# First softmax attention: the factors of every third job ahead of the next job's maxima on VectorE

## The chip, the cores and the metric

One Trainium2 chip, one core of it. The kernel runs the whole computation in one launch. The metric is the device time of one execution in microseconds (us); smaller is better. The core has TensorE (matmuls and transposes), VectorE, ScalarE, GpSimd, and SyncE, which here issues the DMAs. Each engine works through its own queue in order; they wait for each other by semaphores.

## The reference

A block of two mixer layers (256 tokens, width 1024) and a second block with two other attentions and a feed-forward part. What matters here is layer 0, a sparse attention with 16 heads of 64 and 4 key groups:

```python
o_cmp = softmax over 15 compressed keys
o_slc = softmax over the selected blocks      # 256 tokens: all 4 blocks are selected, so causal
o_win = softmax over a window of 512          # 256 tokens: causal
o = gates[0] * o_cmp + gates[1] * o_slc + gates[2] * o_win
return (o * silu(z)) @ w_out
```

So two causal softmax attentions over 256 keys (two "branches") and a small one, gated and added. Then follow `x = x + y`, the norm and layer 1.

## The kernel before, in words

Every weight goes from memory into a raw buffer (SyncE's queue), is split by ScalarE into a high half (`w_hi`, L1242) and by VectorE into the rest (`w_lo`, L1688), and TensorE does three matmuls for each product (L458 to L460).

The first softmax attention (`attention`, called between the gate projection `a_z` and the output projection `a_out`) is cut into 24 jobs, `JOBS`. Three jobs belong to each pair of heads: tokens 128 to 255 for branch 0, the same for branch 1, and tokens 0 to 127 for both branches. A job fills one PSUM bank of 512 columns: two rows of 256 keys in the first two kinds, four rows of 128 keys in the third (job numbers j with j % 3 == 2). It goes through these steps; the letters are used throughout:

- S(j), TensorE, L601 and L604: scores into a bank. It waits until the exponentials of job j-3 or so have left the bank.
- M(j), VectorE, L1805: the negated row maxima, one reduction of 512 columns.
- E(j), ScalarE, L1345: two exponentials of 256 columns, or four of 128 in each third job, each with a read of its accumulated sum.
- F(j), VectorE, L1815 and L1817: the factors, a reciprocal of the sums and a product with the gates (2 or 4 columns).
- W(j), GpSimd, L2446: the probabilities times the factors, 512 columns.
- T(j), TensorE, L616: four transposes; then a copy out of PSUM, by ScalarE (L1335) for two jobs of three and by VectorE (L1872) for the third.
- V(j), TensorE, L650: probabilities times values, two jobs at a time.

All engines run the same loop over turns j. In turn j TensorE issues S(j), T(j-3) and in every second turn two V. ScalarE issues the copy of job j-3 and then E(j). VectorE issues M(j) first and then F(j-1), and behind them what else stands in that turn: the compressed branch's softmax (L1826 to L1845, in turns 0 to 5), the copy of its transposed weights (L1866), the copy of each third job (L1872), the gated output (L1790) and its rest half (L1795) once in six turns, and the split of a weight piece (L1688) in a few turns. The order is written by hand, and no scheduler changes it. GpSimd issues only the W, in order.

What each engine waits for around the change: M(j) for S(j) (`s_ready`), E(j) for M(j) (`s_max`) and for T(j-3), whose buffer it takes, F(j) for E(j) (`p_exp`), W(j) for F(j) (`p_fac`), T(j) for W(j) (`p_ready`). In ScalarE's queue these lines hold it:

```python
act.wait_ge(S["s_max"], j + 1)
if j >= 3:
    act.wait_ge(S["pt_ps"], j - 2)
```

Of the kernel before, what the change touches and what calls it, by code (L numbers as in the profile page):

```python
# [152 lines left out]
def program(nc, io, out):  # L153
# [7 lines left out]
    with ExitStack() as ctx:  # L161
# [177 lines left out]
        def bc(ap, shape, at):  # L339
            return ap.unsqueeze(at).broadcast_to(shape)  # L340
# [9 lines left out]
        NJ = len(JOBS)  # L350
# [4 lines left out]
        def z_done(j):  # L355
            return 5 + min(max(j - 7, 0) // 3, 3)
# [6 lines left out]
        def score_bank(j):  # L363
            return ps[2 + j % 2 if j < J4 else (j - J4) % 4]
# [4 lines left out]
        def quad_at(j):  # L369
            q, r = divmod(j - JQ - LAG - 1, JQ)  # L370
            return q if r == 0 and 0 <= q < 4 else None
# [1298 lines left out]
        def _(dve):  # L1670
# [4 lines left out]
            def link(ins):  # L1675

                chain[0] += 1
                ins.then_inc(S["dve"], 1)
                dve.wait_ge(S["dve"], chain[0])

            def split_lo_to(n):

                while nxt[0] < min(n, NSUB):
                    s = nxt[0]
                    dve.wait_ge(S["hi_ready"], s + 1)
                    if slot_free(s):
                        dve.wait_ge(S["sub_used"], slot_free(s))
                    V.tensor_tensor(split(w_lo, s), rawsub(s)[0], split(w_hi, s).bitcast(F), ALU.subtract).then_inc(S["lo_ready"], 1)  # L1688
                    nxt[0] += 1
# [90 lines left out]
            def z_gate(phase, f):  # L1780

                dve.wait_ge(S["z_t"], 8 * phase + f + 1)
                V.scalar_tensor_tensor(out=zs[:, f, :], in0=zs[:, f, :], scalar=1.0, in1=z_bank(phase, f)[:, 0:T], op0=ALU.add, op1=ALU.mult)\
                    .then_inc(S["z_free"], 1)

            def gated(q):

                o = ps[6 + q % 2][:, :].rearrange("p (a n) -> p a n", a=2)
                g = og[:, 2 * q:2 * q + 2, :]
                V.tensor_tensor(g, o, zs[:, 2 * q:2 * q + 2, :], ALU.mult).then_inc(S["og_ready"], 1)  # L1790

            def output_lo(phase, q):
                dve.wait_ge(S["ot_hi"], 4 * phase + q + 1)
                for f in (2 * q, 2 * q + 1):
                    V.tensor_tensor(tok_tiles(1, f), og[:, f, :].rearrange("p (a b) -> p a b", b=P), tok_tiles(0, f).bitcast(F), ALU.subtract)\  # L1795
                        .then_inc(S["ot_lo" if f % 2 else "dve"], 1)
                chain[0] += 1

            def attention(z0):

                def maxima(j):
                    qt, heads, brs = JOBS[j]
                    nb, c = 4 // (qt + 1), 4 * (j % 8)
                    dve.wait_ge(S["s_ready"], j + 1)
                    V.tensor_reduce(nmax[:, c:c + nb], score_bank(j)[:, :].rearrange("p (r n) -> p r n", r=nb), X, ALU.max, negate=True)\  # L1805
                        .then_inc(S["s_max"], 1)

                def factors(j):

                    qt, heads, brs = JOBS[j]  # L1810
                    nb, c = 4 // (qt + 1), 4 * (j % 8)
                    dve.wait_ge(S["p_exp"], j + 1)
                    f, sm_ = facs[:, c:c + nb], sums[:, c:c + nb]
                    h = heads[0]
                    link(V.reciprocal(f, sm_))  # L1815
                    fv = f.rearrange("p (h b) -> p h b", b=len(brs))
                    V.tensor_tensor(fv, fv, gate[:, qt, 1 + brs[0]:2 + brs[-1], h:h + 2].rearrange("p b h -> p h b"), ALU.mult).then_inc(S["p_fac"], 1)  # L1817

                pcv = pc.rearrange("p (h c) -> p h c", c=16)

                def compressed_sums():
                    dve.wait_ge(S["cm_s"], 1)
                    for qt in range(2):
                        hi_s, lo_s = (ps[4 + qt][:, :].rearrange("p (h i c) -> p h i c", h=NH, i=2)[:, :, i] for i in range(2))
                        o = pc[:, T * qt:T * qt + T].rearrange("p (h c) -> p h c", c=16)
                        link(V.tensor_tensor(o, hi_s, bc(cst[:, C_CB + 16 * qt:C_CB + 16 * qt + 16], [P, 16, 16], 1), ALU.add))  # L1826
                        link(V.tensor_tensor(o, o, lo_s, ALU.add))

                def compressed_maxima():
                    link(V.tensor_reduce(cmx, pcv, X, ALU.max))  # L1830

                def compressed_shift():
                    V.tensor_tensor(pcv, pcv, bc(cmx, [P, 32, 16], 2), ALU.subtract).then_inc(S["cm_sub"], 1)

                def compressed_factors():
                    dve.wait_ge(S["cm_exp"], 1)
                    link(V.tensor_reduce(csum, pcv, X, ALU.add))
                    link(V.reciprocal(cf0, csum))
                    for qt in range(2):
                        some_seen = cst[:, C_CM + 16 * qt:C_CM + 16 * qt + 1]  # L1840
                        f = cf0[:, NH * qt:NH * qt + NH]
                        link(V.scalar_tensor_tensor(out=f, in0=f, scalar=some_seen, in1=gate[:, qt, 0, :], op0=ALU.mult, op1=ALU.mult))

                def compressed_weights():
                    V.tensor_tensor(pcv, pcv, bc(cf0, [P, 32, 16], 2), ALU.mult).then_inc(S["cm_p"], 1)  # L1845

                for j in range(NJ + LAG + 3):
                    if j < NJ:
                        maxima(j)
                    if 1 <= j <= NJ:  # L1850
                        factors(j - 1)
                    if j in (1, 3):
                        z_gate(0, 6 + j // 2)
                    if j == 0:
                        compressed_sums()
                    elif j == 1:
                        compressed_maxima()
                    elif j == 2:
                        compressed_shift()
                    elif j == 4:  # L1860
                        compressed_factors()
                    elif j == 5:
                        compressed_weights()
                    if j == 7:
                        dve.wait_ge(S["cm_pt"], 1)
                        V.tensor_copy(pcT, ps[5][:, :]).then_inc(S["cm_ptsb"], 1)  # L1866
                    v = j - LAG
                    if 0 <= v < NJ and v % 3 == 2:
                        dve.wait_ge(S["pt_ps"], v + 1)
                        if v >= 4:  # L1870
                            dve.wait_ge(S["pv"], v - 3)
                        V.tensor_copy(xn[:, 512 * (v % 4):512 * (v % 4) + 512], ps[4 + v % 2][:, :]).then_inc(S["pt_dve"], 1)  # L1872
                    q = quad_at(j)
                    if q is not None:
                        if q == 0:
                            dve.wait_ge(S["z_free"], 8)
                        dve.wait_ge(S["pv"], JQ * (q + 1))
                        gated(q)
                    q = quad_at(j - 1)
                    if q is not None:  # L1880
                        output_lo(0, q)
                    split_lo_to(z0 + z_done(j - 1) + RING)
# [212 lines left out]
            split_lo_to(za + 9)  # L2095
            z_gate(0, 5)
            attention(za)
            norm_stage(1, first["a_out"])

# [438 lines left out]
```

## Time and profile before

| | |
|---|---|
| median of 3 runs | 792.64 us (792.53 to 792.73) |
| the profiled execution | 793.19 us |
| its span, first to last instruction | 791.3 us |
| granted TensorE clock, mean | 0.999 |
| TensorE busy | 773.3 us, 98% |
| VectorE busy | 545.6 us, 69% |
| ScalarE busy | 423.4 us, 54% |
| GpSimd busy | 109.2 us, 14% |

The first attention takes about 53 us of the span, from S(0) at 105.5 us to the last V at 159.0 us. The chain of waits, followed back from the last instruction, is TensorE's for 83% of the span and VectorE's for 8%. Rows of the timeline give start and duration of an instruction, and in brackets how long its engine had been idle before it and who ended that.

### The profile page before, as it was taken

Reading aid. Unit: us, or ns where it says so; the run is one execution under the profiler, and the core shown is the slowest. Engines: PE = TensorE matmul, PEld = TensorE weight load, DVE = VectorE, ACT = ScalarE, POOL = GpSimd, SP = SyncE. Lnnn points to the kernel's source line nnn. Section 1 sums busy time; section 2 is a strip of 40 time slices with the busy share of each in tenths; the row PEclk is TensorE's granted clock in tenths of the full one; section 3 lists DMA queues with packets and bytes.
Section 4 is the critical chain, followed back from the end, with each engine's and each line's share of the span. In section 5 each row is a group of like instructions: output and inputs, shape, how many; then the busy total and the mean of one; then the engine's idle time right before and its main releaser. Section 6 shows DMA issues by size and latency. Waiting matters only on the chain.

```text
span 791.3 us, 13449 instructions
## 1 busy us (share of the span) xinstructions
PE 773.3 (98%) x5250; PEld 678.5 (86%) x5250; DVE 545.6 (69%) x912; ACT 423.4 (54%) x832; POOL 109.2 (14%) x105
## 2 busy tenths in 40 slices
PE   7999999999999999999999999999999999999996
PEld 4888998788998788999977999999987888888885
DVE  5897978857986763449439577778766656666565
ACT  5447557845548644457356355654445444454453
POOL 1344125501725020000000000111001000000000
PEclk9999999999999999999999999999999999999999
DMA  8756311144431543744335443327464555545631
GB/s 298 231 169 214 107 54 54 55 158 145 160 107 55 190 137 125 263 146 128 104 107 191 145 146 107 118 97 236 166 218 153 185 188 195 204 160 197 215 121 53
DMA packets 93106, 120.74 MB, mean 153 GB/s; under 512 B 8490, under 2 KB 69347, under 8 KB 93044
## 3 DMA queue, kind: packets, MB, share of 16 engines
q1 hardware_dynamic: 92176, 117.67, 44.4%
q0 software_dynamic: 432, 1.57, 0.6%
q8 instruction: 42, 0.69, 0.3%
q10 hardware_dynamic: 436, 0.65, 0.2%
q14 instruction: 20, 0.16, 0.1%
HBM read 118.83 MB, written 1.05 MB: 151 GB/s over the span
## 4 chain that ended last, share of the span: by engine, by line
PE 83%; DVE 8%; ACT 4%; issue 2%; POOL 1%; DMA 1%; ACTq 0%; POOLq 0%; DVEq 0%
PE banks L458 19%; PE banks L460 18%; PE banks L459 18%; PE banks L510 9%; PE banks L512 4%; DVE w_lo L1688 3%; PE banks L530 1%; PE banks L650 1%; PE banks L568 1%; PE banks L1091 1%; PE banks L604 1%; ACT w_hi L1242 1%; PE banks L616 1%; DMA cst<-in_c_keep 1%; ACT tmp L1382 1%
## 5 line engine op out<-in xcount | busy, mean ns | idle before, releaser
L1688 DVE TENSOR_TENSOR w_lo<-raw,w_hi 128x1024 fp32r<-128x1024 f32 x210 | 260.7, 1252 | 101.8 <-ACT w_hi L1242 101.3
L1242 ACT CAST w_hi<-raw 128x1024 fp32r<-128x1024 f32 (+1 forms) x211 | 218.5, 1046 | 150.4 <-PE banks L460 116.7
L458 PE MATMUL banks<-h,w_hi 128*128 128x256 f32 (+1 forms) x512 | 149.6, 292 | 0.7 <-DVE ar L2146 0.4
L460 PE MATMUL banks<-h,w_lo 128*128 128x256 f32 (+1 forms) x512 | 145.3, 284 | 0.0
L459 PE MATMUL banks<-h,w_hi 128*128 128x256 f32 (+1 forms) x512 | 145.3, 284 | 0.0
L458 PE MATMUL banks<-w_hi,h 128*128 128x512 f32 (+1 forms) x264 | 104.3, 395 | 0.9 <-DVE h L1695 0.6
L460 PE MATMUL banks<-w_hi,h 128*128 128x512 f32 (+1 forms) x264 | 102.2, 387 | 0.0
L459 PE MATMUL banks<-w_lo,h 128*128 128x512 f32 (+1 forms) x264 | 102.1, 387 | 0.0
L510 PE MATMUL banks<-h,w_hi 128*128 128x512 f32 x288 | 100.5, 398 | 0.0
L458 PEld LDWEIGHTS banks<-h,w_hi 128*128 128x128 f32 x512 | 97.6, 191 | 3.2 <-issue 2.0
L459 PEld LDWEIGHTS banks<-h,w_hi 128*128 128x128 f32 x512 | 97.7, 191 | 0.2
L460 PEld LDWEIGHTS banks<-h,w_lo 128*128 128x128 f32 x512 | 97.6, 191 | 0.0
L512 PE MATMUL banks<-h,w_lo 128*128 128x256 f32 x252 | 70.7, 281 | 0.0
L2419 POOL TENSOR_TENSOR small<-small 128x2 f32<-128x2 f32 (+5 forms) x26 | 26.8, 1030 | 297.0 <-DVE small L2404 184.3
L458 PEld LDWEIGHTS banks<-w_hi,h 128*128 128x128 f32 x264 | 50.2, 190 | 13.1 <-issue 3.0
L510 PEld LDWEIGHTS banks<-h,w_hi 128*128 128x128 f32 x288 | 52.4, 188 | 10.1
L460 PEld LDWEIGHTS banks<-w_hi,h 128*128 128x128 f32 x264 | 50.2, 190 | 10.1
L459 PEld LDWEIGHTS banks<-w_lo,h 128*128 128x128 f32 x264 | 50.3, 190 | 9.2
L512 PEld LDWEIGHTS banks<-h,w_lo 128*128 128x128 f32 x252 | 47.6, 189 | 1.5
L458 PE MATMUL banks<-w_hi,o 128*128 128x512 f32 x88 | 34.4, 391 | 0.3 <-DVE w_lo L1688 0.3
L460 PE MATMUL banks<-w_hi,o 128*128 128x512 f32 x88 | 34.2, 389 | 0.0
L459 PE MATMUL banks<-w_lo,o 128*128 128x512 f32 x88 | 34.2, 389 | 0.0
(352 smaller groups left out, 1359.5 us busy)
## 6 DMA issues: line engine op xcount, KB each, us to landing
raw<-in_w_in SPq DMA_DIRECT2D x24, 1024.0 KB, 5.0
raw<-in_a_w_in SPq DMA_DIRECT2D x13, 1024.0 KB, 5.1
raw<-in_w_ffn_gate SPq DMA_DIRECT2D x11, 1024.0 KB, 5.0
raw<-in_w_ffn_up SPq DMA_DIRECT2D x11, 1024.0 KB, 5.1
raw<-in_w_ffn_down SPq DMA_DIRECT2D x11, 1024.0 KB, 4.9
raw<-in_b_w_in SPq DMA_DIRECT2D x9, 1024.0 KB, 5.0
raw<-in_w_gate SPq DMA_DIRECT2D x8, 1024.0 KB, 5.3
raw<-in_a_w_out SPq DMA_DIRECT2D x4, 1024.0 KB, 4.9
```

The costliest lines, as they stand in the source:

```text
L458: mm(o, lh, rh, start=start, stop=False)
L459: mm(o, lh, rl, start=False, stop=False)
L460: return mm(o, ll, rh, start=False, stop=stop)
L510: last = mm(o, wh[:, kt, :], both(kt), start=kt == 0, stop=kt == KT - 1, skip_group_check=True)
L512: mm(o[:, 0:T], wl[:, kt, :], rhs_h(kt), start=False, stop=False, skip_group_check=True)
L530: last = nc.tensor.transpose(ps[4 + 2 * tt + half][:, P * j:P * j + P], xn[:, a:a + P], ident)
L568: last = nc.tensor.transpose(tbank(phase, e)[:, P * j:P * j + P], t, ident)
L604: last = mm(b[:, wide * i:wide * i + wide], q_st[:, h // 2, h % 2, P * qt:P * qt + P], k[:, h // 4, brs[0]:brs[-1] + 1, 0:w], start=False, ...
L616: last = nc.tensor.transpose(ps[4 + j % 2][:, P * i:P * i + P], tmp[:, 512 * (j % 3) + P * i:512 * (j % 3) + P * i + P], ident)
L1242: nc.scalar.copy(split(w_hi, s), rawsub(s)[0]).then_inc(S["hi_ready"], 1)
L1688: V.tensor_tensor(split(w_lo, s), rawsub(s)[0], split(w_hi, s).bitcast(F), ALU.subtract).then_inc(S["lo_ready"], 1)
L2419: G.tensor_tensor(dst, var, mhalf[0:var.shape[0], 0:n], ALU.pow).then_inc(S[done], 1)
```

## The change

In turns 3, 6, 9, ... 24 VectorE issues F(j-1) ahead of M(j) rather than behind it. F(j-1) is there the factors of a job with four exponentials. In all other turns the order stays M(j), F(j-1). In turn 24 there is no M.

```diff
                 for j in range(NJ + LAG + 3):
+                    if j and j % 3 == 0 and j <= NJ:
+                        factors(j - 1)
                     if j < NJ:
                         maxima(j)
-                    if 1 <= j <= NJ:
+                    if j % 3 and j <= NJ:
                         factors(j - 1)
```

VectorE's queue around turn 15, in the kernel before. The rows are F13, the copy of job 11, the split of a weight piece, M15, F14, M16 and F15:

```order
L1815 RECIPROCAL small<-small 128x2 [waits p_exp]
L1817 TENSOR_TENSOR small<-small 128x2 [waits dve]
L1872 COPY xn<-banks 128x512 [waits pv,pt_ps]
L1688 TENSOR_TENSOR w_lo<-raw,w_hi 128x1024 [waits sub_used,hi_ready]
L1805 TENSOR_REDUCE small<-banks 128x2 [waits s_ready]
L1815 RECIPROCAL small<-small 128x4 [waits p_exp]
L1817 TENSOR_TENSOR small<-small 128x4 [waits dve]
L1805 TENSOR_REDUCE small<-banks 128x2 [waits s_ready]
L1815 RECIPROCAL small<-small 128x2 [waits p_exp]
L1817 TENSOR_TENSOR small<-small 128x2 [waits dve]
```

The same place in the changed kernel (lines below the edit count two more):

```order
L1815 RECIPROCAL small<-small 128x2 [waits p_exp]
L1817 TENSOR_TENSOR small<-small 128x2 [waits dve]
L1874 COPY xn<-banks 128x512 [waits pv,pt_ps]
L1688 TENSOR_TENSOR w_lo<-raw,w_hi 128x1024 [waits sub_used,hi_ready]
L1815 RECIPROCAL small<-small 128x4 [waits p_exp]
L1817 TENSOR_TENSOR small<-small 128x4 [waits dve]
L1805 TENSOR_REDUCE small<-banks 128x2 [waits s_ready] x2
L1815 RECIPROCAL small<-small 128x2 [waits p_exp]
L1817 TENSOR_TENSOR small<-small 128x2 [waits dve]
```

F14, the pair with 128x4, stands ahead of M15, and M15 and M16 follow each other.

VectorE's queue around turn 21, in the kernel before: the copy of job 17, M21, F20, M22, F21 and the gated output of a quarter of the heads:

```order
L1872 COPY xn<-banks 128x512 [waits pv,pt_ps]
L1805 TENSOR_REDUCE small<-banks 128x2 [waits s_ready]
L1815 RECIPROCAL small<-small 128x4 [waits p_exp]
L1817 TENSOR_TENSOR small<-small 128x4 [waits dve]
L1805 TENSOR_REDUCE small<-banks 128x2 [waits s_ready]
L1815 RECIPROCAL small<-small 128x2 [waits p_exp]
L1817 TENSOR_TENSOR small<-small 128x2 [waits dve]
L1790 TENSOR_TENSOR ar<-banks,ar 128x512 [waits pv]
```

The same place in the changed kernel:

```order
L1874 COPY xn<-banks 128x512 [waits pv,pt_ps]
L1815 RECIPROCAL small<-small 128x4 [waits p_exp]
L1817 TENSOR_TENSOR small<-small 128x4 [waits dve]
L1805 TENSOR_REDUCE small<-banks 128x2 [waits s_ready] x2
L1815 RECIPROCAL small<-small 128x2 [waits p_exp]
L1817 TENSOR_TENSOR small<-small 128x2 [waits dve]
L1790 TENSOR_TENSOR ar<-banks,ar 128x512 [waits pv]
```

M21 now stands behind F20, and with it behind the wait for job 20's exponentials.

The queues of TensorE, ScalarE, GpSimd and SyncE are the same in both kernels.

## Rows read from the trace of the kernel before

**Rows 1.** The page: busy time by engine, share of the span, instructions.

```profile
PE 773.3 (98%) x5250; PEld 678.5 (86%) x5250; DVE 545.6 (69%) x912; ACT 423.4 (54%) x832; POOL 109.2 (14%) x105
```

**Rows 2.** Busy time of the stretch: length, PE, PEld, DVE, ACT, POOL, clock, DMA share, GB/s.

```profile
105.00:159.00 54.00, 51.43 (x484) 45.32 (x482) 42.41 (x107) 41.45 (x157) 25.71 (x24) 1.00 0.12 41
```

**Rows 3.** Timeline of TensorE: start, duration, what, idle time before and its releaser.

```profile
121.07 0.63 PE L624 MATMUL banks<-cst,ar 128*128 128x128 f32 x4 [1.36 <-ACT xn L1335]
...
141.26 0.66 PE L616 MATMUL banks<-cst,tmp 128*128 128x128 f32 x4 [0.87 <-POOL tmp L2446]
...
148.86 0.61 PE L616 MATMUL banks<-cst,tmp 128*128 128x128 f32 x4
```

**Rows 4.** The chain of waits, 140 to 160 us: start, duration, what.

```profile
140.17 1.05 POOL tmp L2446
...
151.31 0.69 DVE small L1805
...
155.83 1.05 POOL tmp L2446
```

**Rows 5.** Timeline of ScalarE and VectorE, turns 3, 6 and 9.

```profile
113.89 0.21 ACT L1345 ACTIVATION_READ_ACCUMULATOR tmp<-banks,small 128x1 f32 x1
...
114.07 0.69 DVE L1805 TENSOR_REDUCE small<-banks 128x2 f32<-128x512 f32 x1 [0.64 <-PE banks L604]
...
114.99 0.48 ACT L1345 ACTIVATE tmp<-banks,small 128x256 f32<-128x256 f32 x1
...
120.24 0.21 ACT L1345 ACTIVATION_READ_ACCUMULATOR tmp<-banks,small 128x1 f32 x1
...
120.30 0.68 DVE L1805 TENSOR_REDUCE small<-banks 128x2 f32<-128x512 f32 x1
...
124.83 0.37 ACT L1345 ACTIVATE tmp<-banks,small 128x128 f32<-128x128 f32 x1 [1.16 <-DVE small L1805]
...
128.68 0.59 ACT L1335 COPY xn<-banks 128x512 f32<-128x512 f32 x1 [0.94 <-PE banks L616]
```

**Rows 6.** Timeline of VectorE and ScalarE, turn 12: M12, F11, E12, the copy behind.

```profile
133.47 0.68 DVE L1805 TENSOR_REDUCE small<-banks 128x2 f32<-128x512 f32 x1
134.07 0.16 DVE L1815 RECIPROCAL small<-small 128x4 f32<-128x4 f32 x1
...
134.35 0.68 DVE L1805 TENSOR_REDUCE small<-banks 128x2 f32<-128x512 f32 x1
...
134.19 0.47 ACT L1345 ACTIVATE tmp<-banks,small 128x256 f32<-128x256 f32 x1 [0.65 <-DVE small L1805]
...
135.10 0.58 ACT L1335 COPY xn<-banks 128x512 f32<-128x512 f32 x1
```

**Rows 7.** Timeline of VectorE, turn 15: M15 and F14.

```profile
139.12 0.68 DVE L1805 TENSOR_REDUCE small<-banks 128x2 f32<-128x512 f32 x1
139.72 0.16 DVE L1815 RECIPROCAL small<-small 128x4 f32<-128x4 f32 x1
```

**Rows 8.** Timelines, turn 18: M18, F18, E18, and W17 with W18.

```profile
145.51 0.68 DVE L1805 TENSOR_REDUCE small<-banks 128x2 f32<-128x512 f32 x1
...
147.28 0.17 DVE L1815 RECIPROCAL small<-small 128x2 f32<-128x2 f32 x1 [0.20 <-ACT tmp L1345]
...
146.22 0.47 ACT L1345 ACTIVATE tmp<-banks,small 128x256 f32<-128x256 f32 x1 [0.54 <-DVE small L1805]
...
146.55 2.20 POOL L2446 TENSOR_TENSOR tmp<-tmp,small 128x512 f32<-128x512 f32 x2 [2.71 <-DVE small L1817]
```

**Rows 9.** Timelines of ScalarE and VectorE, turn 21: E20's first and last part, M21, F21.

```profile
148.76 0.37 ACT L1345 ACTIVATE tmp<-banks,small 128x128 f32<-128x128 f32 x1
...
150.05 0.21 ACT L1345 ACTIVATION_READ_ACCUMULATOR tmp<-banks,small 128x1 f32 x1
...
149.56 0.68 DVE L1805 TENSOR_REDUCE small<-banks 128x2 f32<-128x512 f32 x1
...
151.91 0.15 DVE L1815 RECIPROCAL small<-small 128x2 f32<-128x2 f32 x1
```

## The prediction

> **What bounds the kernel now.** First the page. TensorE is busy 98% of the span [rows 1], so time is lost only where TensorE ends up waiting, or where something beside it sets the end of a stretch. Then the table by stretch: the first attention lies at 105 to 159 us, and TensorE is busy 51.43 of 54 us there, 95%, at the full granted clock (1.00) [rows 2]. Third, the timeline of TensorE in that stretch: it stands idle 1.36 us at 121.07, behind the ScalarE copy of job 3, and 0.87 us at 141.26, behind GpSimd's W14 [rows 3]. T18 at 148.86 starts the moment W18 is done: almost no slack. Last, the chain of waits: through 141 to 151 us it runs on TensorE, but at 151.31 it goes over to VectorE (M22) and stays with VectorE and GpSimd up to W23 at 155.83 [rows 4]. So the change, which leaves TensorE's work alone, counts (a) where it moves one of the waits of rows 3, and (b) undiluted at the end, where the chain is VectorE's own queue.
>
> **Unit prices.** An M holds VectorE for 0.60 us and E starts 0.72 us after its M (133.47 to 134.07, and to 134.19) [rows 6]. An F, two tiny instructions, holds VectorE 0.28 us (134.07 to 134.35) [rows 6]. W starts 0.45 us behind its F and takes 1.05 us (139.72, 140.17) [rows 4, 7]. Four exponentials last from 148.76 to 150.05 + 0.21 = 150.26, 1.50 us [rows 9]; two take 1.04 us by the same pattern, and ScalarE is free for the next 0.91 us after their start (134.19 to the copy at 135.10) [rows 6].
>
> **What the change does.** Nothing is added or removed. In turns 3, 6, ... 21 (seven places; in turn 24 there is no M, so nothing moves) F(j-1) goes ahead of M(j). If E(j-1) has ended by then, F comes 0.60 us earlier and M 0.28 later. If not, VectorE now stands and waits for E(j-1), with M(j) queued behind that wait; and since E(j) needs M(j), ScalarE stands too. No DMA is moved; SP's queue is not passed. GpSimd's and ScalarE's orders are as they were. The times below are those of the trace of before plus the shift.
>
> Turn 3: E2 ends at 113.89 + 0.21 = 114.10, and M3 began at 114.07 [rows 5]. Now F2 at 114.13, M3 at 114.41, E3 at 115.13 instead of 114.99 [rows 5]: **0.14 late**. E3, the compressed exponentials, VectorE's compressed factors, M5, E5 and the copy of job 3 follow without a gap up to TensorE's 1.36 us wait [rows 3], so TensorE and all behind it are 0.14 late. I leave this out of the times of the next turns and add it at the end.
>
> Turn 6: E5 ends at 120.24 + 0.21 = 120.45, M6 began at 120.30 [rows 5]. Now M6 at about 120.76, E6 and E7 0.5 to 0.6 late. ScalarE was idle for 1.16 us before E8 [rows 5], which waits for M8, and M8 for TensorE: that swallows it. The copy of the compressed weights, queued behind F6 at 122.34, is as late, and T5 at 123.91 needs it done (123.02): room for 0.9. **Nothing**; without that cover it would cost 0.6. Turn 9: F8 cannot go before E8 has ended (it waited for it before too, at 126.37), so W8 gains nothing and M9, E9 are some 0.7 late; ScalarE's idle 0.94 us before the copy of job 7 [rows 5] swallows that. **Nothing**; uncovered 0.7.
>
> Turn 12: VectorE comes to M12 at 133.47 straight from a weight split, E11 long done. F11 goes first, M12 and E12 are 0.28 late [rows 6]. From E12 on ScalarE has no gap (E12, copy, E13, a weight cast, E14), and VectorE's weight split, which waits for that cast, ends at 139.12 where M15 starts [rows 7]: now 139.40. **0.28 late** on the ScalarE/VectorE side. TensorE's T12 goes 0.27 late with W12, but this is hidden in the 0.87 us wait of T14.
>
> Turn 15: E14 now ends at 139.23, F14 starts at 139.40 instead of 139.72 [rows 7], W14 at 139.85 instead of 140.17, and T14 at 140.94 instead of 141.26: TensorE **gains 0.32**. But M15 is at 139.68, 0.56 late, and so are E15, E16, the cast and the next split. The Trainium skill's page "Perfetto Trace Analysis", section "Optimization Strategy", says to find the gaps on the engine to be filled and "determine how to make those dependencies start sooner". By that rule W14 ought to give up to 0.60 of the 0.87 us gap; the rows give 0.32, and it doesn't stay. It is the third rival below.
>
> Turn 18: VectorE comes to M18 at 145.51 + 0.56 = 146.07; F17 first, M18 at 146.35, E18 at 147.07 (was 146.22): 0.85 late [rows 8]. F17 is no earlier than before. F18, which waits for E18, goes from 147.28 to 148.12 [rows 8]; W18 was right behind W17 and ended at 146.55 + 2.20 = 148.75, and now ends at 148.12 + 0.45 + 1.05 = 149.62. T18 goes from 148.86 to 149.65: TensorE **0.79 late**, the gain is gone. E20 had waited a little for M20; it now starts as soon as E19 leaves ScalarE, at 149.37 instead of 148.76 (0.61 late), and ends at 150.87.
>
> Turn 21: M21 ran at 149.56, in the shadow of E20 [rows 9]. Now F20 waits to 150.90, M21 starts at 151.18 (1.62 late), E21 at 151.90, ending at 152.94. F21, which had run at 151.91 [rows 9], waits for that until 152.97: **1.06 late**. S22 is 0.79 late and gives M22 at 152.10, no later bound. Behind F21 VectorE's queue (gated output, M23, F22, copy, output halves, F23) and then W23 are the chain of waits with nothing in reserve [rows 4], so W23 is at 156.89 and the output projection 1.06 late.
>
> **Sum:** 0.14 + 1.06 = **1.2 us slower**. After the section the projection is bound by TensorE, with the weights fetched ahead, so the delay stays as it is. The profiled execution took 793.19 us for a span of 791.3; I expect a span of 792.5, and 792.64 + 1.2 = 793.84 for the median. The price of an F in a new place is bounded by 0.16 us (one instruction alone) and 0.45 (its whole latency); at three to four turns that count, the sum lies between 0.8 and 1.7; I take 0.28, the measured pitch.
>
> **Rivals.** *Only the end counts:* the slack at turns 12 to 18 is larger than I read, and E20 is on time. Then F20 is at 150.29, M21 at 150.57, E21 ends at 152.33, F21 at 152.36: 0.45 late, with turn 3's 0.14 some 0.6 in all, 793.2. For it: ScalarE's small idle times at M14, M16 and M20; against: the weight cast and split in turns 12 to 17 run without any. *More is lost:* the covers of turns 6 and 9 don't hold. The place is E9: it now ends at about 128.4, and F9 stands at 128.85. From 0.4 us more lateness on, F9 and the chain behind it up to W9 and the splits are late as well, with 0.6 to 0.7 per turn: 1.2 + 0.6 to 1.3 = about 2.2 (1.7 to 2.6), 794.8. For it: VectorE was busy almost to the next M in these turns; against: the two idle times of rows 5. *Faster:* earlier W are what TensorE wants, the 0.87 us gap goes, and the M side is hidden. It would bring 0.3 (turn 15 as worked out) to 0.9 (all of the gap), 792.0. For it: rows 3; against: in turns 9, 18 and 21 F comes no earlier at all, for it is the exponentials it waits for. That the order doesn't come out as the diff says can't be: VectorE runs its queue as written, and the listing shows it.
>
> **How the numbers follow.** Forecast 0.51 (its own range 0.8 to 1.7 us), only the end 0.20, more lost 0.22, faster 0.07. 0.2% is 1.6 us, about what a measurement tells from no change. The forecast lies within it but for a tenth, "only the end" wholly, "more lost" beyond it, and "faster" mostly within, since the gap on TensorE is under 1 us: faster 0.03, same 0.69, slower 0.28. The range leaves out the gain, the low part of "only the end" and the top of "more lost": 792.9 to 795.0.
>
> **What would show it.** In the new profile: M21 about 1.6 us later than before, right after E20's end; ScalarE idle about 0.7 us between the copy of job 18 and E21; T14's wait down from 0.87 to under 0.5 us; a new wait of TensorE of some 0.8 us for W18 before T18; F2 ahead of M3 and E3 0.1 late. Weight splits and matmuls outside the section as before. Wrong would be: T18 on time, M22 still the place where the chain goes over to VectorE, or a shift that differs between W23 and the end of the program.

## The result and the profile after

The changed kernel takes 793.87 us (median of 21 runs, 793.46 to 794.57), the kernel before 792.63 us (21 runs, 792.29 to 793.38). The ratio is 1.0016, with an interval of 1.0011 to 1.0022: 1.2 us slower, and clear of the noise, though under the 0.2% that was called no change.

| | before | after |
|---|---|---|
| median | 792.63 us | 793.87 us |
| span of the profiled execution | 791.3 us | 792.1 us |
| M0, the first maxima of the section | 106.41 | 105.98 |
| W23, the last weighting | 155.83 | 156.67 |
| from M0 to W23 | 49.42 us | 50.69 us |

The two profiled executions don't reach the section at the same time: M0 is 0.43 us earlier in the one after, although nothing ahead of it differs. So all shifts below are counted from M0. From M0 to W23 the changed kernel takes 1.27 us more, and 1.27 - 0.43 = 0.84 is what the spans differ by (0.8). After W23 nothing is added or won back.

The page of the changed kernel, first lines: busy times are those of before [rows 1], to within 0.3 us on each engine.

```profile
span 792.1 us, 13449 instructions
...
PE 773.3 (98%) x5250; PEld 678.2 (86%) x5250; DVE 545.8 (69%) x912; ACT 423.5 (53%) x832; POOL 109.0 (14%) x105
...
PE 81%; DVE 10%; ACT 4%; issue 3%; POOL 1%; DMA 1%; ACTq 0%; POOLq 0%; DVEq 0%
```

The last line is the chain of waits: TensorE's share fell from 83% to 81%, VectorE's rose from 8% to 10%.

Timeline of VectorE and ScalarE in the changed kernel, turns 3 and 9 (they answer to [rows 5]): F2, M3, E3; then F8, M9, E9 and the copy of job 7.

```profile
113.71 0.18 DVE L1815 RECIPROCAL small<-small 128x4 f32<-128x4 f32 x1 [0.71 <-ACT tmp L1345]
...
114.00 0.69 DVE L1805 TENSOR_REDUCE small<-banks 128x2 f32<-128x512 f32 x1
...
114.72 0.47 ACT L1345 ACTIVATE tmp<-banks,small 128x256 f32<-128x256 f32 x1
...
126.10 0.18 DVE L1815 RECIPROCAL small<-small 128x4 f32<-128x4 f32 x1 [0.70 <-ACT tmp L1345]
...
126.39 0.68 DVE L1805 TENSOR_REDUCE small<-banks 128x2 f32<-128x512 f32 x1
...
127.11 0.48 ACT L1345 ACTIVATE tmp<-banks,small 128x256 f32<-128x256 f32 x1 [0.57 <-DVE small L1805]
...
128.41 0.59 ACT L1335 COPY xn<-banks 128x512 f32<-128x512 f32 x1 [0.28 <-PE banks L616]
```

Here is the new wait: VectorE stands 0.70 us at F8 with M9 behind it, then ScalarE stands 0.57 us for M9. But ScalarE still waits 0.28 us for TensorE before the copy of job 7 (0.94 before): the delay stops there.

VectorE, turns 12, 15, 18, and W18 on GpSimd (they answer to [rows 6 to 8]). "x2" is two maxima in a row.

```profile
133.20 0.16 DVE L1815 RECIPROCAL small<-small 128x4 f32<-128x4 f32 x1
133.40 0.17 DVE L1817 TENSOR_TENSOR small<-small 128x4 f32<-128x4 f32 x1
133.48 1.28 DVE L1805 TENSOR_REDUCE small<-banks 128x2 f32<-128x512 f32 x2
...
139.14 0.17 DVE L1815 RECIPROCAL small<-small 128x4 f32<-128x4 f32 x1
139.34 0.17 DVE L1817 TENSOR_TENSOR small<-small 128x4 f32<-128x4 f32 x1
139.42 1.28 DVE L1805 TENSOR_REDUCE small<-banks 128x2 f32<-128x512 f32 x2
...
146.10 1.28 DVE L1805 TENSOR_REDUCE small<-banks 128x2 f32<-128x512 f32 x2
...
148.31 1.04 POOL L2448 TENSOR_TENSOR tmp<-tmp,small 128x512 f32<-128x512 f32 x1 [1.01 <-DVE small L1817]
```

Counted from M0, M12 is 0.44 late, M15 0.73, M18 1.02: 0.29 more each time, on top of the 0.15 of turn 3.

TensorE in the changed kernel (it answers to [rows 3]): the compressed weights, T12, T14, T18.

```profile
120.80 0.63 PE L624 MATMUL banks<-cst,ar 128*128 128x128 f32 x4 [1.47 <-ACT xn L1335]
...
136.79 0.66 PE L616 MATMUL banks<-cst,tmp 128*128 128x128 f32 x4 [0.19 <-POOL tmp L2448]
...
140.68 0.66 PE L616 MATMUL banks<-cst,tmp 128*128 128x128 f32 x4 [0.30 <-POOL tmp L2448]
...
149.40 0.66 PE L616 MATMUL banks<-cst,tmp 128*128 128x128 f32 x4 [0.76 <-POOL tmp L2448]
```

T14's wait is down from 0.87 to 0.30 us, and 0.76 us stand in front of T18, where there was none. Last, pieces of the chain of waits: M10, and then turns 18 to 23 (it answers to [rows 4]; pieces of under 0.1 us are left out between the lines):

```profile
127.97 0.69 DVE small L1805
...
149.01 1.11 ACT tmp L1345 x6
150.14 0.51 ACT tmp L1345 x2
150.67 0.19 DVE small L1815
150.88 0.16 DVE small L1817
151.04 0.61 DVE small L1805
151.71 0.35 issue
152.05 0.32 ACT tmp L1345 x2
...
152.73 0.18 DVE small L1815
...
156.67 1.05 POOL tmp L2448
157.76 0.67 PE banks L616 x4
```

It no longer runs on TensorE up to M22. From M10 at 127.97 us on, all its work up to W23 is ScalarE's and VectorE's; E19 and E20, F20, M21, E21, F21 follow one another. Over the same stretch the chain of before was TensorE's, but for 134.6 to 141.3 us and again from M22 on.

### The profile page after: what moved, and what is told of

The parts are those of the page before. It is cut to its first block, busy times and chain, and to the rows that moved or that the text cites. A ratio compares the mean times of both kernels' runs of the same rounds, so it can differ in the third digit from the quotient of the medians.

```text
span 792.1 us, 13449 instructions
## 1 busy us (share of the span) xinstructions
PE 773.3 (98%) x5250; PEld 678.2 (86%) x5250; DVE 545.8 (69%) x912; ACT 423.5 (53%) x832; POOL 109.0 (14%) x105
## 4 chain that ended last, share of the span: by engine, by line
PE 81%; DVE 10%; ACT 4%; issue 3%; POOL 1%; DMA 1%; ACTq 0%; POOLq 0%; DVEq 0%
PE banks L458 19%; PE banks L460 18%; PE banks L459 18%; PE banks L510 9%; PE banks L512 4%; DVE w_lo L1688 3%; ACT tmp L1345 1%; DVE small L1805 1%; PE banks L568 1%; PE banks L530 1%; PE banks L1091 1%; ACT w_hi L1242 1%; ACT tmp L1382 1%; DMA cst<-in_c_keep 1%; PE banks L857 1%
```

## The experiments

My theory: a swap costs 0.28 us for each M that stands on a chain across VectorE and ScalarE which has no slack (turns 12, 15, 18), and a wait for E20 in turn 21; turns 6 and 9 are covered. The rivals: only the end counts; more is lost, in turns 6 and 9; the earlier W is a gain. Times are medians; "before" in the first four is 792.64 us (33 runs on the same chip), in the last four 792.52 us (23 runs). A change below 0.6 us is hardly told apart by the time alone, so each run's shift at W23, counted from M0, stands beside it. Each such shift is from one profiled execution.

### Turns 3, 6 and 9 only

```diff
-                    if j and j % 3 == 0 and j <= NJ:
+                    if j in (3, 6, 9):
                         factors(j - 1)
...
-                    if j % 3 and j <= NJ:
+                    if 1 <= j <= NJ and not (j in (3, 6, 9)):
                         factors(j - 1)
```

> F goes ahead of M in turns 3, 6 and 9 only. All shifts are counted from M0. My theory (turn 3 costs 0.14, turns 6 and 9 are covered by ScalarE's idle time): M10 and every later step 0.14 to 0.16 us late, M6 about 0.5 and E9 about 0.7 us late without any effect on TensorE, W23 and the time +0.15 us. Rival 'more is lost' (the covers of turns 6 and 9 do not hold): W23 and the time +1 us or more. Rival 'nothing before turn 12 matters': +0.0 everywhere from M10 on.

Measured 792.83 us, ratio 1.0003 (0.9994 to 1.0011). From M0: M6 0.63 late, E9 0.84, M10 0.15, every later M 0.13 to 0.17, W23 (155.95, with M0 at 106.36) 0.17. M10 in the kernel before, then in this run:

```profile
128.25 0.69 DVE L1805 TENSOR_REDUCE small<-banks 128x2 f32<-128x512 f32 x1 [1.50 <-PE banks L604]
...
128.35 0.69 DVE L1805 TENSOR_REDUCE small<-banks 128x2 f32<-128x512 f32 x1 [0.90 <-PE banks L604]
```

So turn 3's delay goes through to the end unchanged, and turns 6 and 9 cost nothing. "More is lost" fell, and so did "nothing before turn 12 matters".

### Turns 12, 15 and 18 only

The same edit with `j in (12, 15, 18)`.

> F ahead of M in turns 12, 15 and 18 only. Theory (from turn 12 on, the loop over VectorE and ScalarE sets the pace, and each M that is put off by one F adds 0.28 us): M15 0.56 late, M18 0.84 late, TensorE's wait before T14 down from 0.87 to about 0.5, a new wait of 0.8 us before T18, W23 and the time +0.8 us. Rival 'only the end counts': T18 less than 0.3 late, and W23 back on time, +0.0. Rival 'faster': the shorter wait before T14 stays as a gain, -0.3 us.

Measured 793.32 us, ratio 1.0010 (1.0001 to 1.0018). From M0: M12 0.30, M15 0.58, M18 0.86, W23 (155.91, M0 at 105.60) 0.89 late. TensorE, T14 and T18:

```profile
140.15 0.66 PE L616 MATMUL banks<-cst,tmp 128*128 128x128 f32 x4 [0.26 <-POOL tmp L2448]
...
148.87 0.66 PE L616 MATMUL banks<-cst,tmp 128*128 128x128 f32 x4 [0.77 <-POOL tmp L2448]
```

The wait before T14 went further down than I wrote (0.26 rather than 0.5), because 0.18 us of it had moved ahead, to T12. "Only the end counts" fell: three swaps in the middle, with turn 21 as before, give more than half of the loss (0.68 of 1.24 us by the medians, 0.89 of 1.27 at W23). "Faster" fell too: T18 is 0.82 late.

### Turn 15 only

The same edit with `j == 15`: the one place where F comes 0.6 us earlier just where TensorE waits for it.

> F ahead of M in turn 15 only. Theory: F14 and W14 0.60 us earlier, TensorE's wait before T14 down from 0.87 to about 0.27 us, so TensorE is 0.6 us early at T14; but M15 is 0.28 late, and with it E15 to E18, so TensorE has lost the 0.6 again by T18, which is 0.25 late, and W23 and the time end at +0.25 us. Rival 'faster': the gain of 0.6 us at T14 stays, time -0.3 to -0.6 us.

Measured 792.86 us, ratio 1.0003 (0.9994 to 1.0012); W23 (155.10, M0 at 105.36) 0.32 late. TensorE's T14 and T17:

```profile
139.63 0.66 PE L616 MATMUL banks<-cst,tmp 128*128 128x128 f32 x4 [0.28 <-POOL tmp L2448]
...
146.90 0.66 PE L616 MATMUL banks<-cst,tmp 128*128 128x128 f32 x4 [0.34 <-POOL tmp L2448]
```

Counted from M0, T14 is 0.58 us early (139.63 - 105.36 = 34.27, against 141.26 - 106.41 = 34.85), and it holds that for three transposes. T17 waits 0.34 us for W17, which is late with M18, and from there on TensorE is behind (T17 0.12, T18 0.26 late). This is the cleanest run against "faster": the gap was filled, and W23 came 0.32 us later, not earlier. The time alone, whose interval runs from 0.5 us faster to 1.0 slower, would not decide it.

### Turn 21 only

The same edit with `j == 21`.

> F ahead of M in turn 21 only. Theory: F20 waits for E20's end, M21 starts about 1.0 us late, E21 0.65 late, F21 and W23 +0.4 us, the time +0.4 us; T18 and everything before turn 21 on time. With the two other runs the parts should add up to the change: 0.15 + 0.8 + 0.4 = 1.35 against 1.2 to 1.3 seen. Rival 'only the end counts': this one alone gives the whole of the change, +1.2 us.

Measured 793.11 us, ratio 1.0006 (0.9997 to 1.0014); W23 (156.13, M0 at 106.23) 0.48 late. VectorE's F20, the maxima M21 and M22, and F21; then ScalarE's E21:

```profile
150.13 0.18 DVE L1815 RECIPROCAL small<-small 128x4 f32<-128x4 f32 x1 [0.64 <-ACT tmp L1345]
...
150.43 1.43 DVE L1805 TENSOR_REDUCE small<-banks 128x2 f32<-128x512 f32 x2
152.20 0.17 DVE L1815 RECIPROCAL small<-small 128x2 f32<-128x2 f32 x1 [0.35 <-ACT tmp L1345]
...
151.14 0.48 ACT L1345 ACTIVATE tmp<-banks,small 128x256 f32<-128x256 f32 x1 [0.57 <-DVE small L1805]
```

With M21 queued behind it, F20 waits 0.64 us for the exponentials, and E21 starts 0.71 late. "Only the end counts" wanted the whole 1.2 us from this run; it gives 0.48.

**Do the parts add up?** 0.17 + 0.89 + 0.48 = 1.54, and the change has 1.27. They don't quite, and the traces show where the 0.27 goes. With turns 12, 15 and 18 swapped, E19 is 0.87 late but E20 only 0.62: E20 had waited for M20 before and so had 0.25 us of slack. In turn 21 E21 adds 0.71, and F21 takes back 0.25, which it had waited for S22's maxima. In the full change that makes 0.16 (turn 3) + 0.62 + 0.71 - 0.25 = 1.24 at F21, and 1.25 is measured. The 0.89 of the run with turns 12 to 18 came over another path, T18 to S22, which the longer one hides.

### The weight splits out of the loop

Why do turns 12 to 18 have no slack, when 6 and 9 have? From turn 11 on VectorE and ScalarE also split weight pieces. Order of before, with those pieces (two casts on ScalarE, three splits on VectorE) behind the last exponentials:

```diff
-                    split_hi_to(z0 + z_done(j) + RING)
+                    split_hi_to(z0 + (8 if j >= 25 else 5) + RING)
...
-                    split_lo_to(z0 + z_done(j - 1) + RING)
+                    split_lo_to(z0 + (7 if j >= 28 else 6 if j >= 26 else 5) + RING)
```

> Order of before (M ahead of F everywhere), but the two weight casts and three weight splits that stood in turns 11 to 17 stand behind the last exponentials (two casts in turn 25, splits in turns 26 and 28 and behind the loop). Theory: the loop over VectorE and ScalarE was as long as TensorE's turn only because of these splits; without them M15 is about 1.8 us earlier, W14 comes in time, TensorE's wait of 0.87 us before T14 is gone, T14 to W23 are 0.9 to 1.0 us earlier, and the time falls by up to 0.9 us, less what the output projection then waits for its weights. Rival 'TensorE alone sets the pace': T14's wait is gone but comes back as another one before turn 22, W23 on time, time +0.0 or more.

Measured 791.39 us (790.98 to 791.85, 11 runs), ratio 0.9985 (0.9977 to 0.9994): faster than both kernels. W23 (154.14, M0 at 105.92) is 1.20 us early, more than the 0.9 to 1.0 I had written. TensorE's T13 and T14, with the last piece of S15 between them: first in the kernel before (T14 stands in [rows 3]), then in this run:

```profile
139.08 0.60 PE L616 MATMUL banks<-cst,tmp 128*128 128x128 f32 x4
...
139.99 0.40 PE L604 MATMUL banks<-o_lo,o 128*128 128x256 f32 x2
...
138.49 0.60 PE L616 MATMUL banks<-cst,tmp 128*128 128x128 f32 x4
...
139.39 0.40 PE L604 MATMUL banks<-o_lo,o 128*128 128x256 f32 x2
139.63 0.60 PE L616 MATMUL banks<-cst,tmp 128*128 128x128 f32 x4
```

T14 follows T13 by 1.14 us; in the kernel before it was 141.26 - 139.08 = 2.18. So that wait had cost 1.04 us of TensorE, 0.17 more than the 0.87 written beside it; T13 itself is 0.10 early. The rows show the 0.17: the 0.87 is counted from the end of S15 as the profile gives it (139.99 + 0.40 = 140.39), but without the wait T14 starts before that end (139.63, against 139.39 + 0.40 = 139.79), since matmuls overlap. The output projection doesn't wait for the postponed pieces: TensorE has no wait listed between the last V and 175 us.

Casts and splits were moved together, so which of them took the slack isn't told apart. One of the splits also took longer than the others in the loop of before, 1.63 us against 1.21; it started while W13 ran on GpSimd (137.08 to 138.12), and M15 stood behind it:

```profile
137.57 1.63 DVE L1688 TENSOR_TENSOR w_lo<-raw,w_hi 128x1024 fp32r<-128x1024 f32 x1
...
144.38 1.21 DVE L1688 TENSOR_TENSOR w_lo<-raw,w_hi 128x1024 fp32r<-128x1024 f32 x1
```

Those 0.42 us may be part of what moving the splits gave back; no run takes them apart from the rest.

### The change on top of that

The seven swaps, in the kernel with late splits.

> The change (seven swaps) on top of the kernel with late splits; to be read against that kernel. Theory: with VectorE and ScalarE having slack in turns 12 to 18, those three swaps cost nothing, as turns 6 and 9 did: T14 and T18 are late only by turn 3's 0.15, and what is left is turn 3 with 0.15 and turn 21 with 0.4 to 0.5, W23 +0.5 to +0.6 us. Rival 'a swap costs 0.28 us wherever it stands': +1.3 us, as in the full change.

Measured 791.99 us, ratio to before 0.9994 (0.9986 to 1.0003); against the kernel with late splits, +0.60 us. W23 (154.78, M0 at 105.93) is 0.63 later than there. T13 and T14, and then VectorE at F20 with M21 and M22 behind it:

```profile
138.66 0.60 PE L616 MATMUL banks<-cst,tmp 128*128 128x128 f32 x4
139.82 0.60 PE L616 MATMUL banks<-cst,tmp 128*128 128x128 f32 x4
...
148.78 0.18 DVE L1815 RECIPROCAL small<-small 128x4 f32<-128x4 f32 x1 [0.70 <-ACT tmp L1345]
...
149.07 1.42 DVE L1805 TENSOR_REDUCE small<-banks 128x2 f32<-128x512 f32 x2
```

T14 is 0.18 late and no more: the three middle swaps, which cost 0.89 us before, cost nothing once VectorE and ScalarE have slack there. What is left is turn 3 (0.16) and turn 21 (0.46). "A swap costs 0.28 wherever it stands" fell, and casts and splits together are shown to be what took the cover away.

### Seven swaps behind jobs with two exponentials

Turns 4, 7, ... 22 in place of 3, 6, ... 21.

```diff
-                    if j and j % 3 == 0 and j <= NJ:
+                    if j > 1 and j % 3 == 1 and j < NJ:
                         factors(j - 1)
...
-                    if j % 3 and j <= NJ:
+                    if 1 <= j <= NJ and not (j > 1 and j % 3 == 1 and j < NJ):
                         factors(j - 1)
```

> Seven swaps again, but in turns 4, 7, ... 22, behind a job with two exponentials. Theory: in those turns VectorE would have reached M(j) while the exponentials of j-1 still run, so nearly each of the seven swaps adds a wait of VectorE for ScalarE; M15 +1.0, T18 +1.6, W23 and the time about +2.5 us, twice the change. Rival 'it is the four exponentials that make the wait': seven swaps behind shorter jobs cost less than the change, under +1.2 us.

Measured 794.77 us (6 runs), ratio 1.0029 (1.0018 to 1.0041), W23 (158.12, M0 at 106.36) 2.34 late. The view of who waited for whom, from 106 to 170 us: total, times, longest. ScalarE waits for the maxima (L1805), VectorE's F (L1815) for ScalarE:

```profile
ACT tmp L1345 <- DVE small L1805: 8.0, 13, 1.2
DVE small L1815 <- ACT tmp L1345: 6.8, 9, 1.0
```

In the kernel before, the same two waits come to 6.1 us in 8 places and 0.8 us in 4. The swaps of turns 7 and 10 cost nothing here; those of turns 13, 16 and 19 put E 0.67 us later each, where those of turns 12, 15 and 18 cost 0.29. So the number of exponentials isn't what makes a swap dear; it is whether VectorE gets to the F before the E is done, and whether a cover comes behind it. The choice of the third jobs was the cheaper one, at the same number of swaps.

### Every turn

F(j-1) ahead of M(j) in all turns.

```diff
-                    if j and j % 3 == 0 and j <= NJ:
+                    if 1 <= j <= NJ:
                         factors(j - 1)
...
-                    if j % 3 and j <= NJ:
+                    if 1 <= j <= NJ and not (1 <= j <= NJ):
                         factors(j - 1)
```

> F(j-1) ahead of M(j) in every turn. Theory: each turn becomes a chain exponentials, F, M, exponentials across ScalarE and VectorE, with no M in the shadow of an E; TensorE waits in most turns, W23 and the time +8 to +9 us. Rival 'costs add by turn': 24 swaps at the change's mean of 0.18 us each, about +4 us.

Measured 800.60 us (4 runs), ratio 1.0099 (1.0084 to 1.0115): +8.1 us; W23 (163.56, M0 at 105.93) 8.21 late. The same two waits, from 106 to 170 us:

```profile
ACT tmp L1345 <- DVE small L1805: 15.2, 21, 1.8
DVE small L1815 <- ACT tmp L1345: 14.4, 18, 1.1
```

No M runs in the shadow of an E any more, and costs don't add by turn: 23 swaps cost six and a half times what 7 do.

## Why the prediction was right

It gave 793.84 us (range 792.9 to 795.0); 793.87 was measured. That the two agree to 0.03 us is luck, for the interval of the measured difference runs from 0.9 to 1.7 us; what can be judged is the path. By its own steps, shifts from M0, turn 3's share included:

| step | predicted | measured |
|---|---|---|
| E3 late | 0.14 | 0.16 |
| E9 late, no effect | 0.84 | 0.85 |
| M12, M15, M18 late | 0.42, 0.70, 0.98 | 0.44, 0.73, 1.02 |
| T14 | 0.18 early | 0.15 early |
| T18 late | 0.93 | 0.97 |
| M21 late | 1.76 | 1.83 |
| F21 late | 1.20 | 1.25 |
| W23 late | 1.20 | 1.27 |

**The price of one place.** 0.28 us for an F was read off one pair of rows [rows 6]; three turns gave 0.29, 0.29, 0.29. The bounds 0.16 and 0.45 were needlessly wide.

**The covers.** Turns 6 and 9 cost nothing, as said. The step on turn 9 put M9 and E9 both at "some 0.7 late"; for M9 that was too little (1.08 beside turn 3's share, since M9 had stood at 125.59 and now waits for E8's end), for E9, which counts, it was right (0.69): E9 had waited for a copy before, not for M9. Of ScalarE's 0.94 us before the copy of job 7, 0.28 are left: the cover held with little to spare, and 0.22 for "more is lost" was a fair worry, though the run with turns 3, 6 and 9 shows nothing of it. In turn 6 the prediction had E6 and E7 both 0.5 to 0.6 late; E6 is (0.48 beside turn 3's share), E7 only 0.22, so part of that delay was gone before ScalarE's idle time ahead of E8.

**The rule that spoke for the change.** The Trainium skill, "Perfetto Trace Analysis", section "Optimization Strategy", asks what the waiting engine waits for, and how to make that start sooner. This case's traces agree for the place, not for the kernel: in the run with turn 15 alone T14's wait falls from 0.87 to 0.28 us, and the kernel is no faster. What was pushed back on the engine that delivers the factors decided it. Here that was M15, and through it E15 to E19.

**What the prediction didn't see.** The chain of waits of before, read as it stood, said TensorE from 141 to 151 us. That was right for that execution and misleading for the change: the path over VectorE and ScalarE ran beside it with almost no slack. Two signs of it stood in the rows: T18 starts 0.11 us behind W18's end, and ScalarE has no gap from E12 to E14. The prediction used both, but its opening took TensorE's waits and the end for the only places that count; the run with late splits shows that 1.2 us of the section were the doing of the casts and splits.

**The 0.2% bound.** 1.2 us is 0.16%. The chances put 0.69 on "within 0.2%", where it fell; with 21 runs on each side the loss is nevertheless clear of noise.

## What to carry to other kernels

Moving a small instruction ahead of another in an engine's queue is not free. What is pushed back comes later by the moved instruction's own time (0.28 to 0.29 us here), and if what the moved one waits for isn't there yet, everything behind it inherits that wait too. Whoever feeds on the instruction pushed back pays. Before filling a gap on the busiest engine, follow the pushed-back instruction forward too, to the next place where its engine and its consumers stand idle: that idle time is the cover, and where none comes before the end of the section, the cost arrives whole and adds up turn by turn. Work with no deadline, such as the splits of weights that are needed only after the loop, belongs behind the loop that has no slack; here that gave back 1.1 us.

## What was unexpected

- Executions reach the section up to 1 us apart, though nothing ahead of it differs: M0 at 106.41 (before), 105.98 (the change), 105.36 (turn 15 only). The spans follow: 791.3, 792.1, 790.6 us. A comparison of spans alone would have put the change at 0.8 us and turn 15 at a gain of 0.7. What the start varies with stays open.
- One wait of TensorE for a transpose's input cost 0.17 us more than the idle time written beside it (1.04 against 0.87 us, T13 to T14 with and without it): that time starts at the end of the matmul before, which the next one otherwise overlaps.
- The sum of the parts was 0.27 us more than the whole. On the path to E21 a slack of 0.25 us before E20 takes up part of the delay of turns 12 to 18; on the path over TensorE, which sets the end when those turns are swapped alone, it does not.
